# A hybrid decoder layer on one core: prompt attention in four pairs, two of its tiles moved behind the first expert gathers

## What is computed

```python
z = modulate(x, norm1_g, sh1, sc1) @ w_in            # q, k, v, gMLP u and v, branch gates
o = attend(q, k, v, lam)                             # two softmax maps per head, A1 - lambda * A2
a_out = rms_norm(o, subln_g) * (1 - lambda_init)
s_out = u * (tril(W_s[g]) v + b[g])                  # per chunk of 128 positions
mix = (ga * (a_out @ w_att_out) + gb * (s_out @ w_gm_out)) @ w_out
x = x + g1 * mix
h = modulate(x, norm2_g, sh2, sc2)
# PEER: 8 heads, 2 x 128 sub-keys, top 16 of each half, top 16 of the 256 sums
top_s, idx = select(h @ w_q, subkeys)                # 128 experts per row
wgt = softmax(top_s) * gelu(sum(h * u_tab[idx]))
x = x + g2 * sum(wgt * v_tab[idx])
```

## Time and profile before

| | us |
|---|---|
| median of 3 runs | 4850.87 (4835.68 to 4861.12) |
| the profiled execution | 4868.02 |
| its span, first to last instruction | 4866.2 |
| PE busy / DVE busy / ACT busy / POOL busy | 2975.9 / 2538.0 / 592.7 / 2711.8 |
| mean DMA rate over the span | 320 GB/s |
| front of the tail | about 885 to 1460 |
| first selection | about 1465 to 1523 |
| tile 0 of the gathers | 1528 to 1785 |
| tiles 1 to 8 | 1785 to the end |

### The profile page before, as it was taken

One profiled execution on the slowest core, in us unless ns is written; L12 is line 12 of the kernel. 1 busy time (PEld: TensorE's weight loads), 2 busy tenths in 40 slices (PEclk: granted clock), 3 DMA queues, 4 the chain that ended last, 5 costly groups with the idle time before them and its releaser, 6 DMA issues.

```text
span 4866.2 us, 47305 instructions
## 1 busy us (share of the span) xinstructions
PE 2975.9 (61%) x16593; PEld 1784.3 (37%) x16593; DVE 2538.0 (52%) x5693; ACT 592.7 (12%) x1228; POOL 2711.8 (56%) x2513
## 2 busy tenths in 40 slices
PE   3889999896892667637567737563455323233344
PEld 1666777564781553314343314341122000000000
DVE  2883150332118887864667765556456456456311
ACT  1111241332111013210013310000000000000000
POOL 2222222233223567766677776667667777777675
PEclk7899999877995887768788868786765655655556
DMA  7223221689866999999999999999999999999898
GB/s 285 75 90 134 95 79 60 241 312 359 337 229 236 396 382 398 337 393 418 419 414 400 370 378 406 420 410 373 389 385 390 377 356 364 379 359 358 332 361 302
DMA packets 481519, 1556.44 MB, mean 320 GB/s; under 512 B 52150, under 2 KB 121207, under 8 KB 465884
## 3 DMA queue, kind: packets, MB, share of 16 engines
q0 software_dynamic: 351376, 1271.99, 67.9%
q1 hardware_dynamic: 129068, 269.21, 14.8%
q10 hardware_dynamic: 864, 12.58, 0.6%
HBM read 1488.47 MB, written 65.23 MB: 319 GB/s over the span
## 4 chain that ended last, share of the span: by engine, by line
POOL 33%; DMA 15%; PE 13%; issue 12%; DVE 5%; another core or an unknown queue 2%; POOLq 1%; ACT 0%; SPq 0%; DVEq 0%; ACTq 0%
POOL v_rows L964 17%; POOL u_rows L955 15%; DMA v_rows<-in_peer_v,expertsT 11%; PE ps_y L1288 5%; DVE u_rows L1857 2%; DMA u_rows<-in_peer_u,experts 2%; DMA v_rows<-in_cache_v 2%; PE ps_bank L1142 2%; PE ps_bank L1066 1%; PE ps_bank L1148 1%; PE ps_y L1247 1%; PE ps_bank L1069 1%; PE ps_y L1206 1%; PE ps_bank L1090 0%
## 5 line engine op out<-in xcount | busy, mean ns | idle before, releaser
L1857 DVE CUSTOM_DVE_ANT_0 u_rows<-u_rows,h_rows 128x1024 f32<-128x1024 f32 x1056 | 1290.6, 1224 | 1157.4 <-DMA u_rows<-in_peer_u,experts 831.0
L1288 PE MATMUL ps_y<-v_rows,w_columns 128*32 128x512 f32 x4224 | 865.7, 952 | 1442.3 <-DMA v_rows<-in_peer_v,expertsT 1329.7
L964 POOL DMA_INDIRECT v_rows<-in_peer_v,expertsT x1056 | 1172.7, 1111 | 604.2 <-issue 288.6
L955 POOL DMA_INDIRECT u_rows<-in_peer_u,experts x1024 | 1119.0, 1093 | 454.1 <-issue 295.5
L1288 PEld LDWEIGHTS ps_y<-v_rows,w_columns 128*32 128x32 f32 x4224 | 171.1, 147 | 1995.3 <-issue 1993.8
L365 PE MATMUL ps_z<-w_in_high,hT_high 128*128 128x512 f32 (+1 forms) x1008 | 401.5, 398 | 29.0 <-ACTq L389 26.7
L365 PE MATMUL ps_z<-w_in_high,hT_low 128*128 128x512 f32 (+1 forms) x1008 | 398.3, 395 | 0.0
L365 PE MATMUL ps_z<-w_in_low,hT_high 128*128 128x512 f32 (+1 forms) x1008 | 397.1, 394 | 0.0
L340 POOL CAST w_in_high<-w_in_buf 128x4096 fp32r<-128x4096 f32 x13 | 47.6, 3661 | 491.3 <-PE ps_z L365 460.7
L1148 PE MATMUL ps_bank<-turned_a,weights 128*128 128x256 f32 (+1 forms) x1280 | 271.9, 373 | 4.2 <-issue 3.3
L1142 PE MATMUL ps_bank<-weights,turned_a 128*128 128x256 f32 (+1 forms) x1152 | 267.0, 391 | 5.9 <-issue 4.0
(11 more groups left out here) (241 smaller groups left out, 3576.0 us busy)
## 6 DMA issues: line engine op xcount, KB each, us to landing
u_rows<-in_cache_kT POOLq DMA_DIRECT2D x128, 512.0 KB, 6.1
v_rows<-in_cache_v POOLq DMA_DIRECT2D x128, 512.0 KB, 6.2
weights<-in_peer_w_q SPq DMA_DIRECT2D x40, 1024.0 KB
w_in_buf<-in_w_in POOLq DMA_DIRECT2D x14, 2048.0 KB, 9.1
scratch_z<-z_out SPq DMA_DIRECT2D x112, 256.0 KB, 2.0
weights<-in_w_att_out SPq DMA_DIRECT2D x20, 1024.0 KB
weights<-in_w_gm_out SPq DMA_DIRECT2D x20, 1024.0 KB
weights<-in_w_out SPq DMA_DIRECT2D x20, 1024.0 KB
```

Of the source, the lines that this page charges most:

```text
L955: pool.indirect_dma_start(ur[:, n % RU, :], None, g.peer_u, bass.IndirectOffsetOnAxis(ap=col, axis=0)).then_inc(s_ur[n % RU], 16)
L964: pool.indirect_dma_start(vr[:, n % RV, :], None, g.peer_v, bass.IndirectOffsetOnAxis(ap=idxT[:, t % 3, k:k + 1], axis=0)).then_inc(s_vr[n ...
L1288: last = nc.tensor.matmul(ps_y[32 * j:32 * (j + 1), b:b + CB], wcol[:, base:base + 32], vr[:, (V0[t] + i + j) % RV, b:b + CB], start=r == ...
L1857: nc.vector.tensor_tensor_reduce(ur[:, n % RU, :], ur[:, n % RU, :], hrow[:, t % 2, :], 1.0, 0.0, ALU.mult, ALU.add, a[:, s:s + 1]).then_i ...
```

## The change

GROUPS_ATT becomes four pairs; the front keeps the attention of tiles 0 and 1 and the first mix, with the same 44 steps of sample attention among 58 steps in place of 74. BACK becomes four stretches of ticks, each with steps spread evenly over it by the new function `timetable`: where there are more steps than ticks, some ticks hold two, and DVE then does two quarters per slot. Attention of the pair (2,3) now stands ahead of mix 1, in ticks 0 to 51. Since mix 1 ends later, tile 1 (LATE) loads the scores of tile 2 in its tick 20 in place of 8 and h of tile 2 in tick 21 in place of 2, and selects in slots 84 to 124, two steps per slot. ScalarE does the columns of the weights (L1455) behind the tick's background step, not ahead of it. The total of attention steps rises from 39 + 23 + 23 to 4 x 23, since each group has seven steps of pipeline.

```diff
-GROUPS_ATT = ((0, 1, 2, 3), (4, 5), (6, 7))
+GROUPS_ATT = ((0, 1), (2, 3), (4, 5), (6, 7))
+def timetable(parts):
+    ticks, slots = {}, {}
+    for steps, begin, end in parts:
+        for i, step in enumerate(steps):
+            ticks.setdefault(begin + i * (end - begin) // len(steps), []).append(step)
+    for tick, steps in ticks.items():
+        for n in range(TICK * len(steps)):
+            slots.setdefault(TICK * tick + n // len(steps), []).append(steps[n // TICK] + (n % TICK,))
+    return ticks, slots
...
-    S0 = 36
+    S0, S1 = 36, 84
...
-    BACK = every("mix", 1) + every("att", 1) + every("mix", 2) + every("att", 2) + every("mix", 3) + every("mix", 4)
+    BACK = ((every("att", 1) + every("mix", 1), 0, 52),
+            (every("att", 2) + every("mix", 2), 52, 104),
+            (every("att", 3) + every("mix", 3), 104, 168),
+            (every("mix", 4), 168, 232))
+    LATE = (1,)
+    AT_TICK, AT_SLOT = timetable(BACK)
...
-                            p = max(0, m - 1)
+                            p = next(n for n, tiles in enumerate(GROUPS_ATT) if tl[0] in tiles)
...
-                        if t * TPT + tick < len(BACK):
-                            kind, p, k = BACK[t * TPT + tick]
+                        for kind, p, k in AT_TICK.get(t * TPT + tick, ()):
                             background[kind](p, k)
-                        if tick == 2 and 1 <= t < PT:
+                        if tick == (21 if t in LATE else 2) and 1 <= t < PT:
                             sp.wait_ge(s_u, U0[t])
                             load_h2(t + 1)
...
-                        if tick == 8:
+                        if tick == (20 if t in LATE else 8):
                             load_scores(t + 1)
...
+                        if t in LATE and tick == 29:
+                            gate_exp(t + 1)
+                        for kind, p, k in AT_TICK.get(t * TPT + tick, ()) if t < PT else ():
+                            background[kind](p, k)
                         if t and tick in (0, 1, 9, 17):
...
-                        if t < PT and S0 <= s < S0 + STEPS:
+                        if t < PT and t not in LATE and S0 <= s < S0 + STEPS:
                             select(t + 1, s - S0)
...
+                        if t in LATE and S1 <= s:
+                            for i in range(2 * (s - S1), min(2 * (s - S1) + 2, STEPS)):
+                                select(t + 1, i)
+                        for kind, p, k, quarter in AT_SLOT.get(t * P + s, ()) if t < PT else ():
+                            background[kind](p, k, quarter)
```

More of the change, by code:

```diff
@@ L599, in tail_phase @@
     place, main, last_in = {}, 0, {}
-    for step in FRONT + BACK:
+    for step in FRONT + [step for steps, _, _ in BACK for step in steps]:
         for key in units(*step):
@@ L1296, in _ @@
                     for tick in range(TPT):
-                        if t < PT and t * TPT + tick < len(BACK):
-                            kind, p, k = BACK[t * TPT + tick]
+                        for kind, p, k in AT_TICK.get(t * TPT + tick, ()) if t < PT else ():
                             background[kind](p, k)
@@ L1467, in _ @@
                                 columns(t - 1, part)
-                        if t < PT and t * TPT + tick < len(BACK):
-                            kind, p, k = BACK[t * TPT + tick]
-                            background[kind](p, k)
                         if t < PT and tick % 4 == 3:
@@ L1474, in _ @@
                             gelu(t, (18, 31).index(tick))
-                        if t < PT and tick == 25:
+                        if t < PT and t not in LATE and tick == 25:
                             gate_exp(t + 1)
@@ L1898, in _ @@
                             weights(t, s // CH - 1)
-                        if t < PT and S0 <= s < S0 + STEPS:
+                        if t < PT and t not in LATE and S0 <= s < S0 + STEPS:
                             select(t + 1, s - S0)
-                        tick = t * TPT + s // TICK
-                        if t < PT and tick < len(BACK):
-                            kind, p, k = BACK[tick]
-                            background[kind](p, k, s % TICK)
+                        if t in LATE and S1 <= s:
[3 more added lines that the diff above has]
+                            background[kind](p, k, quarter)
                     if t < PT:
```

## The result

| | kernel before | changed kernel |
|---|---|---|
| median of the runs | 4841.98 us (13 runs, 4829.75 to 4865.14) | 4864.02 us (13 runs, 4857.17 to 4878.5) |
| ratio | | 1.0052, 95% interval 1.0037 to 1.0066 |
| profiled execution (span) | 4868.02 us (4866.2) | 4863.36 us (4861.3) |
| both once more, in a later set of runs (e5) | 4842.45 us (25 runs) | 4857.98 us (10 runs), 1.0035 (1.0018 to 1.0051) |

The forecast was 4861 us, no change that can be told, range 4805 to 4915. The median is 3 us above it. The change is 0.35 to 0.5% slower: at the upper edge of "no change" in the first set of runs, inside it in the second. Both intervals lie above 1, so the small loss is clear of the noise in both sets.

The account below looks back on a forecast made before the run. It took GpSimd's issuing of expert gathers as the biggest bound, with VectorE binding tile 0. Terms -60 + 40 + 20 + 5 + 5 = +10 us on the profiled 4868.0 gave 4878, scaled by 0.9965 to 4861 us, range 4805 to 4915.

Parts of the forecast that it names:

- part 1: Front: attention of tiles 2 and 3 leaves it, so 575 us becomes 515, -60 us (bounds -91 and -14).
- part 2: Tile 0: the moved attention runs there on VectorE, so 257 us becomes 297, +40 us.
- its idle time of 26 us stays about as it is: Tile 0: VectorE's idle time was taken as unchanged, 270 us of work plus 27 giving 297.
- The lower bound, +25: Tile 0: the low price of the moved attention, if VectorE's idle time falls to 12 us.
- part 3: Tiles 1 to 8: 19 more background steps run there, +20 us (bounds +8 and +30).
- 1.04 us per step: Tiles 1 to 5: price of a background step, from 160 us that the background adds for 154 steps.
- wrong at the root: Named signs: tile 0 not bound by VectorE, or background steps in tiles 1 to 7 clearly off 1 us.
- part 4: Tile 1: selecting for tile 2 late, in slots 84 to 123 at two steps per slot, costs +5 us.
- part 5: Tiles 1 and 3: scores queue behind attention loads, VectorE waits some 4 and 15 us, +5 us for both.
- A: Rival, chance 0.25: front gives back all of TensorE's 91 us, under 495 us; total 4815 us.
- B: Rival, chance 0.18: scores come late, VectorE waits over 25 us at tile 1's slot 84; total 4912 us.
- C: Rival, chance 0.12: front stays at DMA's 310 GB/s, gives back 14 us, over 550 us; total 4907 us.

Follow-up runs that it names:

- e5: The changed kernel once more, unchanged, as a measure for the runs beside it: 4857.98 us, 1.0035 of the kernel before.
- e6: Kernel before with the attention of tiles 0 to 3 split in two pairs, both still in the front, nothing moved: 1.0009 of the kernel before.
- e7: The changed kernel without the attention of tiles 2 and 3, every other step keeping its tick: 0.9962 of the kernel before.
- e2: e1 with an evened timetable: pair (2,3) in ticks 0 to 40, pair (4,5) in 40 to 104: 0.9984 of the kernel before.
- e11: e3 with the last mix's 35 steps in ticks 168 to 186 in place of 168 to 232: 1.0021 of the kernel before.
- e3: e2 with tile 1's selection at one step per slot from slot 36, as in other tiles: 0.9973 of the kernel before.
- e1: The changed kernel with SyncE loading a tile's scores ahead of its tick's attention loads: 1.0004 of the kernel before.
- e4: The changed kernel with another weave in the front, fewer cached pages asked for early and more late: 1.0002 of the kernel before.
- e9: The kernel before with SyncE loading a tile's scores ahead of its tick's other loads: 0.9995 of the kernel before.
- e8: e3 with tile 0's selection run beside the sample attention's last seven steps: 0.9896 of the kernel before, from four runs.

## Why the prediction was right, and where only its sum was

The sum said +10 us, and the move cost 10.3 us between e6 and e5. That is luck: tile 0 came 26 us cheaper than its term, all that stands behind it 29 us dearer, and the two misses cancel. Against the kernel before itself the difference of the medians is 22 us in the first set of runs and 16 in the second.

- **Front (part 1), predicted -60, 515 us.** Measured -65 between the first profiles, -62.6 against e6; 510 us. The step of turning needs into a stage's length by today's filling held. DMA moved 342 GB/s over the stage (376 x 264 + 305 x 246, over 510), where 340 was named. The rule of the Trainium skill (DMA: Bandwidth & Descriptors, section Where 436 GB/s comes from), about 358 GB/s from the HBM side, doesn't bind here: 376 GB/s over 264 us, 403 over tiles 4 and 5.
- **Tile 0 (part 2), predicted +40, 297 us.** Measured +18 in the first profile and +14 in e5. Two steps failed. The smaller is VectorE's work, 270 predicted and 261 found: the attention was to add 54 us and adds 42 by e7, and the durations that were summed overlap a little from one operation to the next in the rows. The larger is "its idle time of 26 us stays about as it is": it fell to 14 and 9 us, since the added work filled waits for rows. The lower bound, +25, had the idle time about right at 12; it was the work that took the tile under it.
- **Tiles 1 to 8 (part 3), predicted +20.** This is the step that missed most: 1.04 us per step was a mean over all kinds of steps, in ticks that never held two, and it was used at a pace of 58 steps in 52 ticks. All parts behind tile 0 were to bring +30; against e6 they brought +59, of it +61 in tiles 1 to 3 with six more steps than before, -14.5 in tiles 4 and 5 with eight fewer, +12.5 in 6 and 7. The last is 0.6 us for each of the 21 steps of the last mix there, about half of the price used. In tiles 1 to 3 steps cost clearly more than 1 us, which the prediction itself had named as a sign of being wrong at the root. The wait that grew there is GpSimd's for TensorE. It does not lie in the doubled ticks alone: by the starts of the dot products, the 86 ticks with one step hold 49 of e5's 61 us (13.15 us each against 12.58 in e6) and the eight with two 19; in the first profile it is 30 and 36. A stop may reach into the ticks behind it, so this says where the time lies and not what caused it. e2 took 46 us back with eleven steps fewer and three doubled ticks in place of eight. How that splits is open: eleven steps at 1.04 us are 11, five doubled ticks by e11's price 2 to 8, and most of it is neither. TensorE's own time, 44 us less in e2, would cover it, and so would in part the 11 MB less that were moved (485 to 474 MB, 27 us at 394 GB/s); a count of steps shows neither.
- **Late selection (part 4), predicted +5.** e2 and e3 differ by nothing in their spans, so its 5 us are not seen.
- **Waits for scores (part 5), predicted +5.** The waits came longer than worked out in both tiles (8.5 and 10.9 us in two profiles against 4; 22 against 15), and by e1 and e4 at most some 10 us of e4's 27 were paid: the ring carried most, as the earlier trace rows had let expect and e9 confirmed.
- **The base.** Scaling the profiled 4868.0 by 0.9965 to the first three runs' median was right in principle. The thirteen runs' median is 4842; on that base the same sum would have given 4852, and 4864 was measured. So 9 of the 12 us that would then be missing were covered by the base, by chance.

**Rivals.** A fell: the front took 510 us and not under 495, and in e4 another weave didn't bring it there either. B fell: VectorE's wait in tile 1 was under 25 us. C fell: 510 us, far under 550. The way it did go, TensorE's queue between v products, was none of the rivals; the prediction had called TensorE's part hidden, and said so only of tile 0, where no v products run.

## What to carry to other kernels

A step of background has no price of its own: in a stage with slack it fills idle time (42 us of VectorE's work cost tile 0 29 us), and where gathers wait behind it for an in-order engine, the same steps cost more when they stand denser (7 to 26 us for 17 doubled ticks in e11). Before moving work, list who stands behind it on each engine's queue in the new place, count the time and the bytes that it adds there and not the steps, and keep the pace at no more than one step per unit of the small, urgent work. A stage that got shorter is worth most when something serial behind it (here a 52 us selection) can then begin earlier: the change alone cost 0.35 to 0.5%, and with an even timetable and an early selection it became 0.7 to 1.0% faster than the kernel before.

## What the hardware showed

GpSimd's time to issue one gather depends on what VectorE is doing when the gather starts. At tile 2's end above it is 0.94 us while VectorE waits (17.28 us in one piece, for TensorE). Right after, with VectorE busy without a gap, it changes from one gather to the next. GpSimd, then VectorE:

```profile
2588.32 1.97 POOL L971 DMA_INDIRECT u_rows<-in_peer_u,experts  x1 [0.30 <-issue]
2590.59 0.94 POOL L980 DMA_INDIRECT v_rows<-in_peer_v,expertsT  x1 [0.30 <-issue]
2591.84 2.00 POOL L971 DMA_INDIRECT u_rows<-in_peer_u,experts  x1 [0.30 <-issue]
```

```profile
2588.25 1.22 DVE L1873 CUSTOM_DVE_ANT_0 u_rows<-u_rows,h_rows 128x1024 f32<-128x1024 f32 x1
2590.54 1.22 DVE L1891 TENSOR_TENSOR y_gated<-ps_y,gate 128x1024 f32<-128x1024 f32 x1
2591.79 1.23 DVE L1893 TENSOR_TENSOR x_then_y<-y_gated,x_then_y 128x1024 f32<-128x1024 f32 x1
```

The two slow gathers start just inside a dot product and just inside an addition of two rows; the fast one starts just inside a product that reads one of its operands from PSUM (`ps_y`). Over tiles 1 to 3 of this profile the same holds: 273 gathers start inside a dot product, and take, at the median, what is left of it and 0.82 us more, up to 2.01 us; 313 start while VectorE is idle and take 0.94 at the median. The Trainium skill (SBUF — State Buffer, section SBUF: two separate sides) says that VectorE can lock GpSimd out of a shared port, so that it can't write descriptors; these rows agree with that, though no run here takes the dot products away.

A stream of large pages can be slow while the DMA engines have room. While e8's selection runs, the sample attention's last value pages come four at a time, each round after the products of the one before, and until the last page is there DMA moves 199 GB/s at a share of 0.57:

```profile
1366.00:1404.00 38.00, 13.79 (x220) 8.56 (x224) 34.95 (x189) 0.00 (x0) 11.76 (x23) 0.54 0.57 199
```

That the six page buffers hold the stream back is argued from this order; no run has more of them.
